# Cross-attention of a hybrid decoder step: softmax in pairs of query tiles, sample values in output partitions of their own, four key tiles behind the queries

## What is computed

```python
def cross_attn(h, mem_k, mem_v, w_xq, w_xo):
    q = (h @ w_xq).reshape(b, L, X_HEADS, X_HEAD_DIM)
    s = jnp.einsum('blhd,bmhd->bhlm', q, mem_k) * (X_HEAD_DIM ** -0.5)
    pr = jax.nn.softmax(s, axis=-1)
    o = jnp.einsum('bhlm,bmhd->blhd', pr, mem_v).reshape(b, L, D_MODEL)
    return o.astype(h.dtype) @ w_xo
```

## Time and profile before

| | |
|---|---|
| median of 3 runs | 1337.98 us |
| lowest, highest | 1337.47, 1340.96 us |
| the profiled execution, its own time | 1335.26 us |
| its span | 1333.5 us |
| PE busy | 1271.6 us, 95% |
| VectorE (DVE) busy | 741.0 us, 56% |
| ScalarE (ACT) busy | 450.8 us, 34% |
| granted PE clock, mean | 0.979 of full |

### The profile page before, as it was taken

The page is one execution under the profiler, slowest core; times in us unless marked ns, Lnnn a source line. Parts: engine busy times, 40 slices in busy tenths (PEclk is TensorE's granted clock), DMA queues, the critical chain, the costliest instruction groups (busy, mean ns, idle before and its releaser), DMA issues.

```text
span 1333.5 us, 23877 instructions
## 1 busy us (share of the span) xinstructions
PE 1271.6 (95%) x9801; PEld 1190.7 (89%) x9801; DVE 741.0 (56%) x1485; ACT 450.8 (34%) x752; POOL 150.9 (11%) x176
## 2 busy tenths in 40 slices
PE   6999999999998999799999997999999999999996
PEld 6999989998887888699999995459999999999995
DVE  5777866656778878863444448323543442433433
ACT  4444533333332135532234233223431331322422
POOL 1000002000114976200010000001000000000000
PEclk7999999999999989899999999999999999999998
DMA  6423322222124666242233639502322222323211
GB/s 222 116 68 90 87 73 67 65 64 64 33 80 141 211 189 188 82 140 86 94 127 131 234 111 337 196 4 64 111 95 80 83 92 95 94 94 95 96 64 64
DMA packets 139214, 147.54 MB, mean 111 GB/s; under 512 B 4210, under 2 KB 132386, under 8 KB 138817
## 3 DMA queue, kind: packets, MB, share of 16 engines
q1 hardware_dynamic: 119124, 126.98, 29.9%
q10 hardware_dynamic: 18096, 8.62, 2.3%
q0 software_dynamic: 1904, 10.65, 2.2%
HBM read 130.21 MB, written 16.68 MB: 110 GB/s over the span
## 4 chain that ended last, share of the span: by engine, by line
PE 85%; DVE 7%; ACT 2%; issue 2%; DMA 2%; POOL 1%; SPq 0%; DVEq 0%; ACTq 0%
PE slot L371 68%; PE slot L1863 2%; PE slot L1774 2%; PE aux L1625 2%; PE aux L1618 1%; PE aux L1619 1%; DVE junk L1388 1%; PE aux L1836 1%; ACT w_hi L349 1%; PE slot L1854 1%; DVE sring L1200 1%; DVE w_lo L356 1%; DMA vr<-in_conv_b 1%; DMA w_raw<-in_w_xo 1%; DVE junk_s L1207 1%
## 5 line engine op out<-in xcount | busy, mean ns | idle before, releaser
L356 DVE TENSOR_TENSOR w_lo<-w_raw,w_hi 128x1024 fp32r<-128x1024 f32 x186 | 232.7, 1251 | 350.0 <-ACT w_hi L349 349.8
L349 ACT ACTIVATE w_hi<-w_raw 128x1024 fp32r<-128x1024 f32 x186 | 196.9, 1059 | 563.0 <-PE slot L371 527.2
L371 PE MATMUL slot<-a_hi,w_hi 128*128 128x260 f32 x1408 | 297.3, 293 | 0.7 <-DVE a_lo L1429 0.7
L371 PE MATMUL slot<-a_hi,w_lo 128*128 128x260 f32 x1408 | 285.0, 284 | 0.0
L371 PE MATMUL slot<-a_lo,w_hi 128*128 128x260 f32 x1408 | 284.5, 284 | 0.0
L371 PEld LDWEIGHTS slot<-a_hi,w_hi 128*128 128x128 f32 x1408 | 221.1, 190 | 16.0 <-issue 12.5
L371 PEld LDWEIGHTS slot<-a_lo,w_hi 128*128 128x128 f32 x1408 | 218.6, 190 | 0.0
L371 PEld LDWEIGHTS slot<-a_hi,w_lo 128*128 128x128 f32 x1408 | 218.4, 190 | 0.0
L371 PE MATMUL slot<-b_hi,w_hi 128*128 128x260 f32 x640 | 129.0, 283 | 1.6 <-DVE gate_b L1259 1.6
L371 PE MATMUL slot<-c_hi,w_hi 128*128 128x260 f32 x640 | 129.4, 283 | 0.2 <-DVE c_lo L1341 0.2
L371 PE MATMUL slot<-b_hi,w_lo 128*128 128x260 f32 x640 | 129.0, 283 | 0.0
(11 more groups left out here) (386 smaller groups left out, 1579.6 us busy)
## 6 DMA issues: line engine op xcount, KB each, us to landing
w_raw<-in_w_in SPq DMA_DIRECT2D x32, 1024.0 KB, 5.8
w_raw<-in_w_up SPq DMA_DIRECT2D x16, 1024.0 KB, 5.3
w_raw<-in_w_down SPq DMA_DIRECT2D x16, 1024.0 KB, 5.1
sring<-in_state_ssm SPq DMA_DIRECT2D x16, 512.0 KB, 4.1
out_ssm_sample<-sring ACTq DMA_DIRECT2D x16, 512.0 KB, 4.0
w_raw<-in_w_ssd_proj SPq DMA_DIRECT2D x8, 1024.0 KB, 5.1
cache<-in_cache_mem_k SPq DMA_DIRECT2D x8, 1024.0 KB, 7.7
cache<-in_cache_mem_v SPq DMA_DIRECT2D x8, 1024.0 KB, 5.0
```

The source lines that it names most:

```text
L349: nc.scalar.activation(w_hi[:, t % 2], w_raw[:, t // 2 % 2, :, t % 2 * P:t % 2 * P + P], ACT.Copy).then_inc(hi_ready, 1)
L356: nc.vector.tensor_tensor(w_lo[:, t % 2], w_raw[:, t // 2 % 2, :, t % 2 * P:t % 2 * P + P], w_hi[:, t % 2].bitcast(F32), ALU.subtract).the ...
L371: last = nc.tensor.matmul(slot[t % 2][:, h, 0:HALF], w[:, t % 2, k, :], act[:, k, h * HALF:(h + 1) * HALF], start=(start and k == 0 and n ...
```

## The change

Four things change.

- The order of tiles becomes K 0 to 3, query 0 to 7, K 4 to 7, V 0 to 7, with the loads in the same order. The last twelve are one loop (MEM_TILES). The 16 half samples of sample score reductions are dealt over its rounds (QK_PIECES), the spreads too (Q_SPREAD). K tiles 4 to 7 are turned into slot banks.
- The softmax works on pairs of query tiles: one row maximum over 2 x 256 scores, one reciprocal for two columns, one copy to probT for both. Scores are made two pairs ahead, and there are four prob buffers instead of two.
- `values_s` writes head h to output partitions 32h to 32h+7 of one PSUM bank. p_diag is ordered by head and sample and filled by one copy; o_tok is one copy of 128 x 256, turned in two transposes. The 16 halves stand in six groups of two or three (S_HALVES), behind scores.
- The first w_xo tile runs as a whole behind the last head's values.

```diff
-T_Q = T_K + 8
-T_V = T_Q + 8
+T_Q = T_K + 4
+T_K2 = T_Q + 8
+T_V = T_K2 + 4
+MEM_TILES = T_XO - T_K2
+QK_PIECES = ((), (0,), (1, 2), (3,), (4, 5), (6,), (7, 8), (9,), (10, 11), (12,), (13, 14), (15,))
+Q_SPREAD = {1: (0, 1), 3: (2,), 4: (3,), 5: (4,), 7: (5,), 8: (6,), 9: (7,)}
+S_HALVES = {1: (0, 1), 2: (2, 3, 4), 3: (5, 6, 7), 4: (8, 9), 5: (10, 11, 12), 6: (13, 14, 15)}
+PAIRS = 2 * XH
...
+            order = [("w_o", u) for u in range(4)] + [("w_xk", 0), ("w_xk", 1)] + [("w_xq", u) for u in range(4)]
+            order += [("w_xk", 2), ("w_xk", 3)] + [("w_xv", u) for u in range(4)] + [("w_xo", u) for u in range(4)]
+            for n, (name, u) in enumerate(order):
+                load_unit(sp, T_O // 2 + n, unit_src(name, u))
+                for c in {("w_xq", 0): (0, 1), ("w_xq", 1): (2, 3), ("w_xv", 1): (4,), ("w_xv", 2): (5, 6), ("w_xv", 3): (7,),
+                          ("w_xo", 0): (8, 9, 10), ("w_xo", 1): (11, 12, 13, 14, 15)}.get((name, u), ()):
+                    load_cache(c)
...
+            for j in range(MEM_TILES):
+                split_lo(dve, T_K2 + j + 2)
+                for piece in QK_PIECES[j]:
+                    scores_s(piece // 2, piece % 2)
...
+            for j in range(MEM_TILES):
+                gemm_mem(T_K2 + j)
...
+                for b in Q_SPREAD.get(j, ()):
+                    spread_q(b)
+                if j in (2, 4):
+                    turn_k(2 + (j - 2) // 2)
+                if j in (6, 8, 10):
+                    turn_v((j - 6) // 2)
+            turn_v(3)
...
-                    last = nc.tensor.matmul(slot[h // 2][0:NS, 1, h % 2 * XD:(h % 2 + 1) * XD], p_diag[:, m, b, h, :],
-                                            cache[n % CR][:, m, h * XD:(h + 1) * XD], start=(b == 0 and m == 0 and h % 2 == 0),
-                                            stop=(b == NS - 1 and m == 1 and h % 2 == 1), skip_group_check=True)
+                    last = nc.tensor.matmul(slot[0][32 * h:32 * h + NS, 1, 0:XD], p_diag[:, m, h, b, :],
+                                            cache[n % CR][:, m, h * XD:(h + 1) * XD], start=(b == 0 and m == 0),
+                                            stop=(b == NS - 1 and m == 1))
...
+            for p in range(PAIRS):
+                turn(p)
+                if p + 2 < PAIRS:
+                    scores(p + 2)
+                if p == 0:
+                    pe.wait_ge(sm_d, 1)
+                    for m in range(2):
+                        last = nc.tensor.transpose(slot[1][:, 1, m * 32:(m + 1) * 32], prob_s[:, m * P:(m + 1) * P], ident[0:32, 0:32])
+                    last.then_inc(sm_e, 1)
+                if p == 1:
+                    pe.wait_ge(sm_f, 1)
+                for half in S_HALVES.get(p, ()):
+                    values_s(half // 2, half % 2)
+                if p % 2 and p < PAIRS - 1:
+                    values(p // 2)
+
+            pe.wait_ge(o_s_row, 1)
...
+            values(XH - 1)
             pe.wait_ge(pv_lo, 6)
             pe.wait_ge(o_s_lo, 1)
-            gemm(pe, T_XO, a_hi, a_lo, kts=range(0, 6))
-            values(3)
-            gemm(pe, T_XO, a_hi, a_lo, kts=range(6, 8), ktwait=lambda kk: pe.wait_ge(pv_lo, kk + 1))
+            gemm(pe, T_XO, a_hi, a_lo, ktwait=lambda kk: pe.wait_ge(pv_lo, kk + 1) if kk >= 6 else None)
```

More of the change, by code:

```diff
@@ L195, in build @@
         junk_s = at("junk_s", [P, 8, N_STATE], R_4N + 16384, BF16)
-        prob = [at(f"prob{k}", [P, MEM], R_4N + 1024 * k) for k in range(2)]
+        prob = [at(f"prob{k}", [P, MEM], R_4N + 1024 * k if k < 2 else R_4N + 10240 + 1024 * (k - 2)) for k in range(4)]
         probT = [at(f"probT{k}", [P, 2, SEQ], R_4N + 2048 + 4096 * k) for k in range(2)]
@@ L1365, in _ @@
             gained_lo(24, 7, CN_X, a_hi, a_lo)
-            for k in range(8):
+            for k in range(4):
                 split_lo(dve, T_K + k + 2)
-                if k == 7:
+                if k == 3:
                     dve.wait_ge(std_ready, 2)
@@ L1393, in row_max, with scores_s @@
[L1393 to L1396, removed]
+            def scores_s(b, m):
+                if m == 0:
+                    dve.wait_ge(qb_mm, b + 1)
+                    dve.wait_ge(cache_in[b % CR], 16 * (b // CR + 1))
+                    if b >= 1:
+                        dve.wait_ge(cache_used, b)
+                for h in range(XH):
+                    c = m * 32 + b * XH + h
+                    ins = nc.vector.tensor_tensor_reduce(junk[:, m, h, :], cache[b % CR][:, m, h * XD:(h + 1) * XD],
+                                                         q_bank(b)[:, h // 2, h % 2 * XD:(h % 2 + 1) * XD], 1.0, 0.0,
+                                                         ALU.mult, ALU.add, s_cols[:, c:c + 1])
+                if m == 1:
+                    ins.then_inc(cache_used, 1)
@@ L1398, in _, with normalise @@
+            def normalise(p):
+                dve.wait_ge(prob_exp, 2 * p + 2)
+                chain(nc.vector.reciprocal(stats[:, 64 + 2 * p:66 + 2 * p], stats[:, 32 + 2 * p:34 + 2 * p]))
+                for n in (2 * p, 2 * p + 1):
+                    nc.vector.tensor_scalar(prob[n % 4][:], prob[n % 4][:], stats[:, 64 + n:65 + n], None, ALU.mult).then_inc(prob_n, 1)
             row_max(0)
@@ L1819, in _ @@
                     last.then_inc(qt_mm, 1)
[L1820 to L1828, removed]
@@ L1829, in _ @@
-            turn_v(3)
[L1831 to L1834, removed]
-                for kk in range(2):
-                    last = nc.tensor.matmul(aux[:, n % 2, 0:MEM], qT[:, 2 * h + kk, tq * P:(tq + 1) * P], kT[:, 2 * h + kk, :],
-                                            start=(kk == 0), stop=(kk == 1))
-                last.then_inc(score_mm, 1)
-            def turn(n):
-                pe.wait_ge(prob_n, n + 1)
-                if n >= 2:
-                    pe.wait_ge(pt_ev, n - 1)
-                for m in range(2):
-                    last = nc.tensor.transpose(aux[:, 2 + n % 2, m * P:(m + 1) * P], prob[n % 2][:, m * P:(m + 1) * P], ident[:])
+                for b in Q_SPREAD.get(j, ()):
+                    spread_q(b)
@@ new lines, in _, with scores @@
+                if j in (2, 4):
+                    turn_k(2 + (j - 2) // 2)
+                if j in (6, 8, 10):
+                    turn_v((j - 6) // 2)
+            turn_v(3)
+            def scores(p):
+                if p >= 2:
+                    pe.wait_ge(prob_exp, 2 * p - 2)
+                for n in (2 * p, 2 * p + 1):
+                    h, tq = n // 4, n % 4
+                    for kk in range(2):
+                        last = nc.tensor.matmul(score_bank(n), qT[:, 2 * h + kk, tq * P:(tq + 1) * P], kT[:, 2 * h + kk, :],
+                                                start=(kk == 0), stop=(kk == 1))
+                    last.then_inc(score_mm, 1)
@@ L1846, in turn @@
+            def turn(p):
+                if p >= 2:
+                    pe.wait_ge(pt_ev, p - 1)
+                for i in range(2):
+                    n = 2 * p + i
+                    pe.wait_ge(prob_n, n + 1)
+                    for m in range(2):
+                        last = nc.tensor.transpose(aux[:, 2 + p % 2, (2 * i + m) * P:(2 * i + m + 1) * P],
+                                                   prob[n % 4][:, m * P:(m + 1) * P], ident[:])
                 last.then_inc(pt_mm, 1)
```

213 lines of the change are left out of this document (105 added, 108 removed).

## The result

The changed kernel takes 1307.8 us (median of 4 runs, 1305.1 to 1310.7) against 1337.7 us: a ratio of 0.977, 95% interval 0.975 to 0.980, 30 us less. The forecast was 1313.6 us with 1309 to 1330 as range. The direction held, and so did the case called likeliest, streams side by side. The size did not: the gain is a fifth larger than forecast, and the median lies 1.2 us under the range.

What follows compares the result with a forecast made beforehand. TensorE (PE), with 85% of the chain of waits, was taken as the bound. G at 818.4 plus 62.0 gave 880.4 against 904.8, 24.4 us less; 1335.3 less 24.4, plus 2.7 to the median, made 1313.6 us, range 1309 to 1330.

Steps and rivals of the forecast that it cites:

- Part A: Tile stretch, four key tiles moved behind the queries: last query tile 12.4 us earlier, last reduction 3.6 us earlier.
- E: End of the last query tile, forecast at 772.8 us instead of 785.2.
- G: End of the last V tile, forecast 45.6 us after E, at 818.4 us.
- Part B: Bridge and attention, pairs with scores two ahead: PE waits of 2.0 and 1.2 us, then PE leads.
- Part C: Sample values in four strips: streams of different heads overlap, 15.1 us instead of 27.6, plus 1.4 for weight-shape changes.
- the rest from G on: PE's work without sample values, 40.5 us, plus waits of 5.0, up to the first w_xo tile's end: 45.5 us.
- the six waits: Tile stretch between E and G: PE waits for VectorE six times, 0.4 to 0.75 us each, 3.3 in all.
- The clock: Behind the bridge: full speed assumed, since PE is never still for over 2 us; a fall would cost 2 to 3.
- Rival 1: Sample values: streams stay one after another and cost 27.6 us, giving 1326.1 us; chance 0.32.
- Rival 2: Tile stretch: weight loads come late and cost 6 to 9 us, giving 1320 to 1323 us; chance 0.06.
- Rival 3: Sample values: switching strips makes each instruction cost 379 ns instead of 216, giving 1347.0 us; chance 0.08.
- Rival 4: Bridge waits and tile stretch stay as VectorE sets them, streams don't overlap: within 4 us of 1338; chance 0.06.

Runs made afterwards that it cites:

- reorder_only: The kernel before with only the new order of tiles, loads, spreads and reductions; 1335.8 us, ratio to before 0.999.
- strips_only: The kernel before with only the heads' sample values in output strips of their own, everything else in the old order; 1328.4 us, ratio 0.993.
- half_reduce: The changed kernel with each of the 64 sample score reductions over 128 instead of 256 elements; 1305.9 us, ratio to before 0.980.
- mid_bridge: The changed kernel with query spreads in mid-tile, first two pairs' scores ahead of V's last turn, first row maximum ahead of the last reductions; 1309.6 us.
- no_reorder: The changed kernel with the old order of tiles and loads, pairs and four strips kept; 1310.0 us, ratio to before 0.982.
- pairs_only: The kernel before with only the softmax pairs, scores two ahead and larger groups, all heads in one strip; 1328.7 us, ratio 0.994.

## Why the prediction was right or wrong

By its own steps, on the profiles of both kernels, first key tile to first w_xo tile:

| step | forecast, us | measured, us |
|---|---|---|
| Part A, last query tile earlier | 12.4 | 11.9 |
| Part A, from there (E) to the end of the last memory tile (G) | 45.6 | 48.2 |
| last reduction behind G | 4.2 | 4.6 |
| Part B, first and second probabilities behind G | 7.7, 11.65 | 7.8, 11.8 |
| Part C, sample values with changes of shape | 16.5 | 8.0 |
| the rest from G on | 45.5 | 45.7 |
| whole | 24.4 less | 29.5 less |

**Part C failed, by 8.5 us, and it put the time out of the range.** The mechanism was right: strips of their own let streams run side by side, shown by one, two and four strips. The mis-sized term is the 15.1 us for the sample values, 16.5 with the changes of shape, where 8.0 were measured. It was wrong because I let a head's second matmul block the head behind it and called the time that follows a lower bound. A quarter of 27.6 us, 6.9, would have been the bound of four strips; the groups take 2 x 0.98 + 4 x 1.41 = 7.6 and gaps behind them 0.4. With 6.9 in place of 15.1 the sum would have been 1305.4, 2.4 under the median. The Trainium skill's 2.38 for three column groups (TensorE: Matmul & The Clock Gate, Part 3) pointed to the better side; measured here are 5.28/1.41 = 3.7 for four groups and 2.0 for two.

**Part A failed too, and in the other direction.** The twelve tiles' 2.6 us too little are the spreads: eight at 0.5 were put in, while one alone costs 0.72 and 0.2 in the tile behind it, and the first two together 1.1 and 0.2: 6 x 0.92 + 1.3 = 6.8 instead of 4.0. I had taken the pipeline off a duration, where the chain of the kernel before, read at its first spread, would have shown the distance:

```profile
790.94 0.72 PE aux L1824 x2
791.67 3.08 PE slot L1774 x24
```

One of the two turns of K stood behind the last query tile already, 0.44. The tail is 0.4 longer than forecast, as the last reduction's row in the changed kernel shows (G is 826.37):

```profile
830.90 0.08 DVE L1421 DVE_READ_ACCUMULATOR2_ANT s_cols<- 128x1 f32 x1
```

Together this eats the 3.6 us that the reductions were to end earlier: 12.4 - 11.9 + 2.6 + 0.4 = 3.5. reorder_only shows it as a whole: nothing gained. That the six waits come to 3.3 was right, and both kernels without them confirm it.

**The two errors partly cancel.** C gained 8.5 us more than forecast, and A and the rest from G on 3.3 less, which is the 5 us between 24.4 and 29.5. That the forecast lay only 5.8 us above the median is in part luck.

**Part B** was right to 0.1 us at both waits of the bridge, and the order at its end came out as said. What the prediction missed is that B and C need each other: it priced C as if it were additive, which could be done only because B was in the same change (strips_only gained 11.2 us, with B there were 19.6).

**The clock** stayed full, as assumed, but the reason given, that PE is never still for over 2 us, doesn't tell the cases apart. PE's waits in the bridge of the kernel before, where it fell, are no longer than that:

```profile
PE slot L1876 <- DVE s_cols L1388: 1.9, 1, 1.9
PE slot L1880 <- DVE prob_s L1406: 1.8, 1, 1.8
PE slot L1863 <- DVE p_diag L1411: 1.3, 1, 1.3
```

half_reduce, with waits of 1.5, 1.9 and 1.2 us against 1.5, 1.9 and 1.35 in the changed kernel, lost it. So its staying up is not sure in every kernel of this shape, and what decides it stays open; in half_reduce's bridge the fall cost 2.4 us.

**The rivals.** Rival 1 is refuted by the four matmuls that start together; its time was met by the kernel that has one strip. Rival 2 didn't come: the changed kernel's list of waits has none of ScalarE for w_xv (mid_bridge's profile has one of 4.1 us, so it can happen). Rival 3 is refuted: matmuls in different strips start within 0.02 us of each other and don't cost 379 ns each. Rival 4 is refuted as a whole; only its tile stretch, which gains nothing, came out so.

## What to carry to other kernels

A row of matmuls with 8 weight columns cost about a quarter here (1.41 instead of 5.28 us for 24) when their outputs lay in four different sets of 32 partitions. Look for such rows in an attention for few tokens, and bound their cost by the fullest strip. The stage in which two engines go in step wasn't shortened by spreading the same work over more tiles: sum the work of both in the new stretch with distances between starts, not with durations less a pipeline. And when one engine's work shrinks fourfold, the chain that it covered (here the softmax of one tile ahead) can become the bound: 8 of the strips' 20 us needed part B, the softmax in pairs with scores two pairs ahead.

## What the runs showed of the hardware that I had not expected

- Two matmuls of one head, in the same strip, don't hold up the next head's: 24 in 1.41 us. Runs of four in one strip don't either (16 in 1.00 us), runs of six do (24 in 2.71 us).
- Two spread matmuls of 512 columns with 16 rows take 0.72 us on the chain and make the tile behind them 0.2 us longer, also where PE didn't wait.
- The clock can fall in a bridge with nearly the same gaps as one in which it stays: 0.50 in half_reduce from 830 to 835 us, 1.00 in the changed kernel. It can fall in one profile and not in another at the same code: 0.57 in no_reorder from 795 to 799 us, 1.00 at the same place in pairs_only.
- A table load of 1.28 us stands in front of the first exponential, directly behind ScalarE's last copy: hidden in the changed kernel, on the chain in mid_bridge.
